# One root for two norms, and activation rows at one byte distance from the weights, in a fused two-model kernel

## The chip, the cores and the metric

The kernel runs on one core of a Trainium2 chip, in one launch. The metric is device time in microseconds, the median of several runs; lower is better.

## The reference

Two small transformers run one after the other on 256 tokens of width 1024, in float32. The first has two layers: MLA and stick-breaking attention in layer 0, chunked band attention in layer 1, each followed by a SwiGLU of inner width 2816, and at the end its final norm. The second puts 16 meta tokens in front (272 columns), has one layer with a gated depthwise convolution and a sparse attention side by side, and then an FFN with a 3-tap convolution. What matters here:

```python
def rms_norm(x, g):
    return x * rsqrt(mean(x * x) + EPS) * g

def reference(...):
    x = first_block(...)          # ends in rms_norm(h, g_final)
    return second_block(x, ...)
def second_block(x, meta_tokens, ...):
    stream = concat([meta_tokens, x])
    h = rms_norm_2(stream, mix_norm_g[0])
    proj = h @ w_in[0]
    ...
    stream = stream + (g_a * y_a + g_b * y_b) @ w_merge_out[0]
```

So between the last down projection of the first model and the first projection of the second lie two norms in a row: the final norm, whose result also is the residual stream, and the mixer's norm of that stream.

## The kernel before, in words

Activations are kept transposed: 8 k tiles of 128 features by 256 (or 258, or 272) tokens. Every product is made of three fp32r matmuls, in `product` (L541 to L543): high part of the weights by high part of the activations, high by low, low by high. Weights come in units of 256 output columns, 8 k tiles of 1024 bytes a partition: SyncE loads a unit into one of four `raw` slots, ScalarE rounds it to `w_hi` (L364), VectorE subtracts to get `w_lo` (L380; in the mixer POOL does so in four parts, L392), two units ahead of TensorE. A unit takes 48 matmuls, 2 tiles by 8 k tiles by 3; a down unit 36 or 30.

The stages stand in the program one after another and each engine has its own stream, ordered by hand in numbered slots: block 0 (in-projections and attention, out-projection, 22 gate/up units, 16 down units), block 1 likewise with 12 QKV units, then the mixer (25 units), `wo`, `pw`, `merge`, 22 FFN units, 16 down units. In the stages whose functions are `ffn_pe` and `down_pe` TensorE runs products without other work between; in the attention stages short steps of the attention are put between every few k tiles.

Activation operands are `u_hi`, `u_lo` (gate/up, QKV, mixer, `pw`, `merge`), `a_hi`, `a_lo` (down), `o_hi`, `o_lo` and `o3_hi`, `o3_lo` (out-projections of blocks 0 and 1), `lat_hi`, `lat_lo` (MLA latents). Between the last down stage of block 1 and the mixer the streams are: `residual_dve` scales and adds the down tiles to `h` (L812, L817), ScalarE squares them (L858), POOL folds two of four pairs (L467), TensorE sums over features with a matrix of ones (`square_sums`, L476), ScalarE makes the root by Ln and Exp (L431, L434), VectorE norms `h` in place (L517), ScalarE squares the eight rows again (L418), TensorE sums those (`norm_pe`, L450), ScalarE makes the second root, and VectorE and ScalarE then make `u_hi` and `u_lo` tile by tile (L517, L443, L510), the first mixer unit following tile by tile.

Where tiles lie in a partition follows from the sizes in order of allocation, each rounded up to 32 bytes. Modulo 256 bytes all weight tiles start at 128. The rows that are the moving operand lie:

| operand | row pitch before | start before | distance from the weights before | pitch after | distance after |
|---|---|---|---|---|---|
| `u_hi`, `u_lo`, 256 columns | 1088 | 128 | 0, 64, 128, 192, then again | 1024 | 192 |
| the same, 258 and 272 columns | 1088 | 128 | as above | 1280 (`m_hi`, `m_lo`) | 192 |
| mixer, query and gate units | 1088 | 184 | 56, 120, 184, 248 | 1280 | 248 |
| mixer, "qi" units | 1088 | 192 | 64, 128, 192, 0 | 1280 | 0 |
| `o_hi`, `o_lo`, `o3_hi`, `o3_lo` | 1024 | 192 | 64 | 1024 | 192 |
| `a_hi`, `a_lo` | 1024 | 64 | 192 | 1024 | 192 |
| `lat_hi`, `lat_lo` | 1024 | 64 | 192 | 1024 | 192 |

In some units (values of attention) the activations are the stationary operand and the weights move.

## Time and profile before

| | |
|---|---|
| median of 3 runs | 1136.59 us (1134.62 to 1137.52) |
| the profiled execution, time | 1133.53 us |
| its span | 1131.7 us |
| TensorE matmul busy | 1092.2 us, 97% |
| VectorE, ScalarE, POOL busy | 66%, 51%, 19% |
| three lines of `product`, `u` operands | busy 517.2, 510.7 and 510.2 us, 1800 matmuls each |
| stages (us from the span's start) | block 0 in 11 to 132, out-projection to 143, gate/up to 270, down to 330; block 1 attention to 450, gate/up to 577, down to 637; mixer 650 to 846; wo, pw, merge to 926; FFN 932 to 1060, down to 1121 |

Matmuls overlap: one lasts some 280 ns while the next begins after some 118 ns, so the time of a stage is the number of its matmuls by the spacing of their starts, and the duration of one is a finer gauge of the same thing. A window of the trace that lies inside a stage gives the spacing: its length by the matmuls in it.

### The profile page before, as it was taken

To read this page: it belongs to the slowest core of one execution; us is meant where nothing else is said; L and a number is where in the kernel's file an instruction comes from. 1 tells how busy PE (TensorE), PEld (TensorE's weight loads), DVE (VectorE), ACT (ScalarE), POOL (GpSimd) and SP (SyncE) were. 2 spreads that over 40 slices of the span, in tenths; PEclk is the share of its full clock that TensorE was granted. 3 is DMA by queue.
4 is the path that set the end of the run, shared out by engine and by line. 5 is a ranking of instruction groups with operands and counts; after the bars stand their busy time and mean duration, and the time that the engine had idled before them with its cause. 6 is when DMAs were issued, how large, how long until landed. Compare 5 with 4: busy or idle time off the path is not lost.

```text
span 1131.7 us, 22236 instructions
## 1 busy us (share of the span) xinstructions
PE 1092.2 (97%) x8781; PEld 1064.6 (94%) x8781; DVE 748.5 (66%) x1229; ACT 577.6 (51%) x847; POOL 215.5 (19%) x198
## 2 busy tenths in 40 slices
PE   7998999999999999999999799999999989999998
PEld 7997899999999999999999799998899989999997
DVE  6776566555657776556555549997886647788653
ACT  5666554444544564544444444446666346655542
POOL 1432030000222110300000067775550000000000
PEclk9999999999999999999999989999999999999999
DMA  8744256555775433566456534454335444465461
GB/s 265 212 114 136 74 179 194 185 167 186 231 242 178 141 122 112 163 200 194 153 182 200 155 112 149 133 167 126 102 122 174 149 149 150 150 197 174 133 201 38
DMA packets 187925, 181.36 MB, mean 160 GB/s; under 512 B 17935, under 2 KB 186268, under 8 KB 187851
## 3 DMA queue, kind: packets, MB, share of 16 engines
q1 hardware_dynamic: 187323, 178.23, 50.0%
q0 software_dynamic: 528, 2.10, 0.6%
q8 instruction: 51, 0.84, 0.3%
q14 instruction: 23, 0.19, 0.1%
HBM read 179.27 MB, written 1.05 MB: 159 GB/s over the span
## 4 chain that ended last, share of the span: by engine, by line
PE 87%; ACT 5%; DVE 3%; POOL 3%; issue 2%; DMA 0%; SPq 0%; ACTq 0%; POOLq 0%; DVEq 0%
PE ps L541 26%; PE ps L542 26%; PE ps L543 26%; POOL work L467 2%; ACT w_hi L364 2%; POOL w_lo L392 1%; PE ps L2008 1%; PE ps L2070 1%; PE ps L450 1%; PE ps L1890 1%; PE ps L2077 0%; PE ps L1897 0%; DVE work L517 0%; DVE w_lo L380 0%; PE ps L1909 0%
## 5 line engine op out<-in xcount | busy, mean ns | idle before, releaser
L541 PE MATMUL ps<-u_hi,w_hi 128*128 128x256 f32 (+2 forms) x1800 | 517.2, 287 | 13.9 <-DVE u_lo L510 6.9
L542 PE MATMUL ps<-u_lo,w_hi 128*128 128x256 f32 (+2 forms) x1800 | 510.7, 284 | 0.0
L543 PE MATMUL ps<-u_hi,w_lo 128*128 128x256 f32 (+2 forms) x1800 | 510.2, 283 | 0.0
L380 DVE TENSOR_TENSOR w_lo<-raw,w_hi 128x2048 fp32r<-128x2048 f32 (+3 forms) x157 | 326.5, 2090 | 143.6 <-ACT w_hi L364 143.3
L541 PEld LDWEIGHTS ps<-u_hi,w_hi 128*128 128x128 f32 x1800 | 343.1, 191 | 17.2 <-issue 13.3
L543 PEld LDWEIGHTS ps<-u_hi,w_lo 128*128 128x128 f32 x1800 | 343.2, 191 | 0.0
L542 PEld LDWEIGHTS ps<-u_lo,w_hi 128*128 128x128 f32 x1800 | 342.5, 190 | 0.8
L364 ACT ACTIVATE w_hi<-raw 128x2048 fp32r<-128x2048 f32 (+3 forms) x182 | 316.3, 1753 | 39.6 <-PE ps L543 29.7
L541 PE MATMUL ps<-a_hi,w_hi 128*128 128x256 f32 x528 | 146.0, 276 | 0.0
L542 PE MATMUL ps<-a_lo,w_hi 128*128 128x256 f32 x528 | 145.9, 276 | 0.0
L543 PE MATMUL ps<-a_hi,w_lo 128*128 128x256 f32 x528 | 145.8, 276 | 0.0
L392 POOL TENSOR_TENSOR w_lo<-raw,w_hi 128x512 fp32r<-128x512 f32 (+1 forms) x100 | 125.2, 1284 | 80.1 <-ACT w_hi L364 63.5
L467 POOL TENSOR_TENSOR work<-work 128x512 f32<-128x512 f32 (+1 forms) x15 | 30.5, 2032 | 542.0 <-ACT work L858 444.7
L541 PEld LDWEIGHTS ps<-a_hi,w_hi 128*128 128x128 f32 x528 | 99.1, 188 | 0.2 <-DVE w_lo L380 0.2
L542 PEld LDWEIGHTS ps<-a_lo,w_hi 128*128 128x128 f32 x528 | 99.2, 188 | 0.0
L543 PEld LDWEIGHTS ps<-a_hi,w_lo 128*128 128x128 f32 x528 | 99.1, 188 | 0.0
L2481 DVE SCALAR_TENSOR_TENSOR ps<-cin,conv_w,ps 128x256 f32<-128x256 f32 x224 | 92.6, 480 | 0.0
L541 PE MATMUL ps<-o_hi,w_hi 128*128 128x256 f32 (+1 forms) x192 | 56.2, 293 | 1.5 <-POOL w_lo L392 0.7
L542 PE MATMUL ps<-o_lo,w_hi 128*128 128x256 f32 (+1 forms) x192 | 54.0, 281 | 0.0
L543 PE MATMUL ps<-o_hi,w_lo 128*128 128x256 f32 (+1 forms) x192 | 54.0, 281 | 0.0
L910 ACT ACTIVATE a_hi<-act_a 128x512 f32 (+1 forms) x22 | 13.9, 632 | 66.5 <-DVE act_a L934 66.5
L858 ACT ACTIVATE work<-h (+2 forms) x32 | 12.0, 413 | 69.9 <-DVE h L817 69.7
(327 smaller groups left out, 1311.1 us busy)
## 6 DMA issues: line engine op xcount, KB each, us to landing
raw<-in_w_in SPq DMA_DIRECT2D x24, 1024.0 KB, 5.3
raw<-in_w_gate SPq DMA_DIRECT2D x22, 1024.0 KB, 5.3
raw<-in_w_up SPq DMA_DIRECT2D x22, 1024.0 KB, 5.4
raw<-in_ffn_up SPq DMA_DIRECT2D x22, 1024.0 KB, 5.1
raw<-in_w_down SPq DMA_DIRECT2D x16, 768.0 KB, 4.4
raw<-in_od_w_qkv SPq DMA_DIRECT2D x12, 1024.0 KB, 5.2
raw<-in_w_down SPq DMA_DIRECT2D x16, 640.0 KB, 4.2
raw<-in_ev_w_in SPq DMA_DIRECT2D x7, 1024.0 KB, 10.1
```

Of the source, the lines that this page charges most:

```text
L364: nc.scalar.activation(w_hi[t % RING][:, 0:n], raw[t % RAW][:, 0:n], ACT.Copy).then_inc(hi_done, 1)
L380: nc.vector.tensor_tensor(w_lo[t % RING][:, 0:n], raw[t % RAW][:, 0:n], w_hi[t % RING][:, 0:n].bitcast(F32), ALU.subtract).then_inc(lo_don ...
L392: a = nc.gpsimd.tensor_tensor(w_lo[t % RING][:, cols], raw[t % RAW][:, cols], w_hi[t % RING][:, cols].bitcast(F32), ALU.subtract)
L450: mm = nc.tensor.matmul(ps[:, bank, 0:n], ones, work[:, kt, 0:n], start=kt == 0, stop=kt == nk - 1)
L467: nc.gpsimd.tensor_tensor(first, first, paired(work)[:, j, :, 0:n], ALU.add).then_inc(sem("sq_folded"), 1)
L541: nc.tensor.matmul(out_ap, a_h, b_h, start=start and n == 0, stop=False)
L542: nc.tensor.matmul(out_ap, a_h, b_l, start=False, stop=False)
L543: mm = nc.tensor.matmul(out_ap, a_l, b_h, start=False, stop=stop and n == len(pairs) - 1)
L858: nc.scalar.activation(paired(work)[:, j, t, 0:n], paired(h)[:, j, t, cols], ACT.Square)\
L910: nc.scalar.activation(paired(a_hi)[:, j], act_a[:, s], ACT.Copy).then_inc(sem("ffn_hi"), 1)
L1890: nc.tensor.matmul(ck_bank(n)[:, P:CK_W], q_pad_c[:, n % 4, P:T1], k_c[:, n // 2, :], start=True, stop=True)\
L2481: nc.vector.scalar_tensor_tensor(out=ends if w == taps else own, in0=cin[:, tile, w + META:w + T2], scalar=conv_w[:, tile, w:w + 1], in1=e ...
```

## The change

It has two parts.

Layout. `u_hi` and `u_lo` get rows of 256 columns (1024 bytes); the same memory is used under other names, `m_hi` and `m_lo`, with rows of 320 columns (1280 bytes) wherever 258 or 272 columns are used. Small unused tiles (`u_place`, `scope_place`, `o_place`, `o3_place`) shift starts so that the distances of the table result. To make room, `x_root` and `q_pad` and two of the 16 heads of the bias table go to the leftovers of the `m` rows, `cva` and `cvb` to `work`, `ki` to `rstd`, `first_cols` to `log_ms`; `act_g` and `act_a` become halves of `acts`.

```diff
+U_PITCH, U_SHIFT = 320, 48
+SHIFT = 16
...
-    u_hi = sb("u_hi", [P, KT, T2], F32R)
-    u_lo = sb("u_lo", [P, KT, T2], F32R)
+    sb("u_place", [P, U_SHIFT])
+    with ExitStack() as t:
+        u_hi = sb("u_hi", [P, KT, T1], F32R, scope=t)
+        hi_rest = sb("hi_rest", [P, KT * (U_PITCH - T1)], scope=t)
+        u_lo = sb("u_lo", [P, KT, T1], F32R, scope=t)
+        lo_rest = sb("lo_rest", [P, KT * (U_PITCH - T1)], scope=t)
+    m_hi = sb("m_hi", [P, KT, U_PITCH], F32R)
+    m_lo = sb("m_lo", [P, KT, U_PITCH], F32R)
...
+    sb("scope_place", [P, SHIFT])
...
+        sb("o_place", [P, 2 * SHIFT], scope=s)
...
+        sb("o3_place", [P, 2 * SHIFT], scope=s)
...
     def u_h(n):
-        return lambda kt: u_hi[:, kt, 0:n]
+        return lambda kt: (u_hi if n == T1 else m_hi)[:, kt, 0:n]
```

Norms. The sum over squares is taken once, of `h` before the final norm with the final gain in the square's scale; its root, with epsilon squared added, gives the mixer's input from `h` directly, with the product of both gains. The plain root and the normed `h` are made too, behind the mixer's input. Meta tokens, which have no final norm, are handled in 16 columns of their own.

```diff
         def squares(j, t):
+            if ph is ph_down1:
+                nc.scalar.activation(paired(work)[:, j, t, META:T2], paired(h)[:, j, t, cols], ACT.Square,
+                                     scale=root_scale[:, bass.ds(j * 2 + t, 1)]).then_inc(sem("sq_done"), 1)
+                return
...
+                for t in range(2 if ph is ph_down1 else 0):
+                    nc.scalar.activation(paired(acts)[:, j, t, :], paired(h)[:, j, t, cols], ACT.Square)\
+                        .then_inc(sem("plain_sq"), 1)
...
-        fold_squares("final", T1)
+        fold_squares("mix2", T2)
+        for j in (1, 2):
+            pool.wait_ge(sem("plain_sq"), 2 * j + 2)
+            wait(pool, sem("plain_folded"), j - 1)
+            first = paired(acts)[:, 0]
+            nc.gpsimd.tensor_tensor(first, first, paired(acts)[:, j], ALU.add).then_inc(sem("plain_folded"), 1)
...
+        nc.scalar.activation(root_scale[:], gains[:, at:at + KT], ACT.Square).then_inc(sem("scale_step"), 1)
+        act.wait_ge(sem("scale_step"), 1)
+        nc.scalar.activation(root_scale[:], root_scale[:], ACT.Ln, bias=eps[:, 0:1]).then_inc(sem("scale_step"), 1)
+        act.wait_ge(sem("scale_step"), 2)
+        nc.scalar.activation(root_scale[:], root_scale[:], ACT.Exp, scale=0.5).then_inc(sem("scale_step"), 1)
+        act.wait_ge(sem("ffn_lo"), 2 + FFN["ffn1"] + FT // 2)
+        nc.scalar.activation(work[:, :, 0:META], h[:, :, 0:META], ACT.Square).then_inc(sem("scale_step"), 1)
+        act.wait_ge(sem("scale_step"), 4)
         residual_act(ph_down1, C1, group=4)
-        norm_finish_act("final", KT, C1, D)
-        for kt in range(KT):
-            act.wait_ge(sem("un_done"), norm_at["final"][1] + kt + 1)
-            square(h[:, kt, :], kt, T2)
-        norm_finish_act("mix2", KT, C2, D, (u_h(T2),))
...
+        both_roots()
+        norm_round_act(norm_at["mix2"][1], KT, T2, u_h(T2))
+        plain_root()
...
-        square_sums("final", T1)
-        pe.wait_ge(sem("rstd_done"), norm_at["final"][0] + 1)
-        norm_pe("mix2", KT, T2)
+        square_sums("mix2", T2)
+        pe.wait_ge(sem("plain_folded"), 2)
+        pe.wait_ge(sem("plain_sq"), KT)
+        pairs_read(pe, ph_down1)
+        for n, kt in enumerate((0, 1, KT - 2, KT - 1)):
+            mm = nc.tensor.matmul(ps[:, 6, 0:T1], ones, acts[:, kt, :], start=n == 0, stop=n == 3)
+        mm.then_inc(sem("ss_done"), 1)
...
-        norm_dve("final", h_at(C1), ("final", 0), KT, T1, into=h_at(C1))
-        dve.wait_ge(sem("un_done"), norm_at["final"][1] + KT)
-        norm_dve("mix2", h_at(C2), ("mix2", 0), KT, T2, (u_h(T2), u_l(T2)))
```

VectorE, from the end of the down stage to the mixer's first steps, before:

```order
L517 SCALAR_TENSOR_TENSOR h<-h,gains,rstd 128x256 x8
L517 SCALAR_TENSOR_TENSOR work<-h,gains,rstd 128x272 x2
L510 TENSOR_TENSOR u_lo<-work,u_hi 128x272
L517 SCALAR_TENSOR_TENSOR work<-h,gains,rstd 128x272
...
L510 TENSOR_TENSOR u_lo<-work,u_hi 128x272 x2
L2497 TENSOR_TENSOR cin<-ps,sg 128x272 x2
```

The same place after the change (`m_lo` takes the place of `u_lo`, and `log_ms` holds the plain root):

```order
L2529 TENSOR_TENSOR work<-meta_gained,rstd 128x8x16
L2531 SCALAR_TENSOR_TENSOR work<-h,both_gains,rstd 128x256 x2
L2524 TENSOR_TENSOR m_lo<-work,m_hi 128x272
L2531 SCALAR_TENSOR_TENSOR work<-h,both_gains,rstd 128x256
...
L2524 TENSOR_TENSOR m_lo<-work,m_hi 128x272 x2
L2539 SCALAR_TENSOR_TENSOR h<-h,gains,log_ms 128x256 x8
L2577 TENSOR_TENSOR cin<-ps,sg 128x272 x2
```

The eight norms of `h` moved from ahead of the mixer's input to behind it, and stand now in front of the first `cin`; one small multiplication for the meta columns was added.

ScalarE at the same place, before:

```order
L431 ACTIVATE log_ms<-ps,eps 128x256
L434 ACTIVATE rstd<-log_ms 128x256
L418 ACTIVATE work<-h 128x272 x8
L431 ACTIVATE log_ms<-ps,eps 128x272
L434 ACTIVATE rstd<-log_ms 128x272
L443 ACTIVATE u_hi<-work 128x272 x8
L364 ACTIVATE w_hi<-raw 128x1088
```

After, with the sigmoids of the first unit's tiles (`sg`) at the end:

```order
L1482 ACTIVATE log_ms<-ps,eps 128x256
L1483 ACTIVATE log_ms<-ps,eps 128x16
L1486 ACTIVATE rstd<-log_ms 128x272
L456 ACTIVATE m_hi<-work 128x272 x8
L1492 ACTIVATE log_ms<-ps,eps 128x256
L1495 ACTIVATE log_ms<-log_ms 128x256
L377 ACTIVATE w_hi<-raw 128x1088
L1523 ACT_TABLE_LOAD
L1523 ACTIVATE sg<-ps 128x272 x2
```

The eight squares in the gap are gone, and one Ln and Exp moved behind the rounding, ahead of the next split and the sigmoids.

## Rows read from the trace of the kernel before

**Rows 1.** The page: the span; busy time, share and instructions of each engine.
```profile
span 1131.7 us, 22236 instructions
...
PE 1092.2 (97%) x8781; PEld 1064.6 (94%) x8781; DVE 748.5 (66%) x1229; ACT 577.6 (51%) x847; POOL 215.5 (19%) x198
```

**Rows 2.** Windows: block 0 gate/up, block 0 down, second model's gate/up.
```profile
core 0: us, PE busy (x) PEld busy (x) DVE busy (x) ACT busy (x) POOL busy (x), PEclk, DMA share, GB/s
160.00:260.00 100.00, 100.00 (x850) 100.00 (x849) 59.29 (x46) 43.90 (x36) 0.00 (x0) 1.00 0.54 169
272.00:322.00 50.00, 50.00 (x443) 50.00 (x442) 31.83 (x33) 26.05 (x28) 8.56 (x4) 1.00 0.73 235
...
937.00:1057.00 120.00, 120.00 (x1003) 120.00 (x1001) 93.96 (x122) 71.61 (x85) 0.00 (x0) 1.00 0.51 164
```

**Rows 3.** Line L542 by window: count, duration ns min/median/max, first and last start us.
```profile
L542 PE MATMUL ps<-lat_lo,w_hi x26: 276/276/283, 77.5 to 93.8; 128*128 128x256 f32 x26
...
L542 PE MATMUL ps<-o_lo,w_hi x29: 280/280/280, 132.8 to 142.7; 128*128 128x256 f32 x29
...
L542 PE MATMUL ps<-u_lo,w_hi x283: 274/282/283, 159.8 to 259.7; 128*128 128x256 f32 x142
...
L542 PE MATMUL ps<-a_lo,w_hi x147: 276/276/276, 272.0 to 321.7; 128*128 128x256 f32 x147
...
L542 PE MATMUL ps<-u_lo,w_hi x334: 277/282/294, 937.0 to 1056.9; 128*128 128x258 f32 x167
...
L542 PE MATMUL ps<-a_lo,w_hi x24: 277/281/281, 1060.5 to 1068.6; 128*128 128x256 f32 x24
...
L542 PE MATMUL ps<-a_lo,w_hi x148: 276/276/276, 1069.9 to 1119.9; 128*128 128x256 f32 x148
```

**Rows 4.** The chain that ended last, from the first sums to the mixer: start, us, what.
```profile
638.93 1.15 PE ps L476 x4
640.08 0.02 issue
640.10 0.48 ACT log_ms L431
...
640.61 0.42 ACT rstd L434
...
642.15 5.61 PE ps L450 x16
...
648.74 0.03 issue
...
650.42 0.36 PE ps L541
```

**Rows 5.** Timeline of VectorE, the final norm of `h`.
```profile
641.06 3.25 DVE L517 SCALAR_TENSOR_TENSOR h<-h,gains,rstd 128x256 f32<-128x256 f32 x8 [2.48 <-ACT rstd L434]
```

**Rows 6.** Windows: a stretch of the second sums.
```profile
642.50:645.90 3.40, 3.40 (x9) 2.59 (x8) 1.81 (x5) 2.27 (x6) 0.00 (x0) 0.50 0.02 5
```

**Rows 7.** Matmuls by line and form over the whole run: busy us, mean ns.
```profile
L542 PE MATMUL ps<-u_lo,w_hi 128*128 128x256 f32 x976 | 275.2, 282 | 0.0
...
L542 PE MATMUL ps<-u_lo,w_hi 128*128 128x258 f32 x672 | 191.7, 285 | 0.0
...
L543 PE MATMUL ps<-u_hi,w_lo 128*128 128x272 f32 x152 | 43.9, 289 | 0.0
...
L542 PE MATMUL ps<-o_lo,w_hi 128*128 128x256 f32 x128 | 35.9, 281 | 0.0
...
L542 PE MATMUL ps<-w_lo,u_hi 128*128 128x256 f32 x112 | 31.4, 280 | 0.0
```

**Rows 8.** Timeline of VectorE and ScalarE at the mixer's second unit.
```profile
659.75 0.44 DVE L2497 TENSOR_TENSOR cin<-ps,sg 128x272 f32<-128x272 f32 x1 [4.30 <-PE ps L543]
...
657.29 0.69 ACT L1469 ACTIVATE sg<-ps 128x272 f32<-128x272 f32 x2
```

**Rows 9.** Timeline of VectorE, the first splits of block 1's down stage.
```profile
581.29 4.56 DVE L380 TENSOR_TENSOR w_lo<-raw,w_hi 128x1280 fp32r<-128x1280 f32 x3 [1.90 <-ACT w_hi L364]
```

**Rows 10.** Timeline of VectorE at the end of the mixer.
```profile
843.93 0.87 DVE L2481 SCALAR_TENSOR_TENSOR work<-cin,conv_w,ps 128x256 f32<-128x256 f32 x2
...
852.30 0.70 DVE L2657 TENSOR_TENSOR gates<-ps,gates 128x516 f32<-128x516 f32 x1 [2.21 <-PE ps L543]
```

118 lines of the change are left out of this document (82 added, 36 removed).

## The prediction

> **What bounds the kernel now.** Start with the page: TensorE is busy in 97% of the span, at a granted clock near full; VectorE has a third of its time free, ScalarE a half [rows 1]. So two things can shorten this kernel: fewer nanoseconds per matmul, and fewer microseconds in which TensorE has no product to work on.
>
> For the first, read windows that lie inside one stage. A window counts about two matmuls more than begin in it. In the first block's gate/up stage 848 begin in 100 us, 117.9 ns from one to the next; in its down stage 441 in 50 us, 113.4 ns; in the last gate/up stage, with 258 columns instead of 256, 1001 in 120 us, 119.9 ns [rows 2]. Clock 1.00 in all three, weights of the same form, both engines of the split with room. DMA is busier in the quicker stage (0.73 against 0.54), so DMA isn't what slows the other.
>
> Then look at single matmuls. In the down stage every one lasts 276 ns; in gate/up the median is 282; the first out-projection has 280 for all; the 26 of the latent stage go from 276 to 283 with a median of 276; the last down stage opens at 281 and is at 276 later [rows 3]. A duration stands 163 ns above its spacing, so 276 is 113.4 and 281 is 118. What differs is where the moving rows lie. By the table above, rows of `a_hi` and `lat_hi` keep 192 bytes (modulo 256) from the weights; those of `u_hi` step through 0, 64, 128, 192 with the k tile; those of `o_hi` keep 64. The 276 appears without scatter in long stages only at the constant 192. But the last down stage opens in the 118 ns rhythm at that same distance: the constant 192 makes the 113 ns rhythm possible and does not guarantee it.
>
> For the second, the chain of waits between the first model's last down stage and the last mixer: sums end at 640.08, the final norm's root is made, eight rows of `h` are normed and squared, eight sums follow, a second root, and the first product starts at 650.42 [rows 4, 5]. A clock of 0.50 lies over 3.4 us of those sums [rows 6].
>
> **The change, term by term.**
>
> *256-column products of gate/up, blocks one and two.* 2 stages x 22 units x 48 = 2112 matmuls, at distance 192 with rows of 1024 bytes, as in the down stage. 117.9 - 113.4 = 4.5 ns each, 9.5 us. Down stages spent about 72 of 1584 matmuls in the 118 ns rhythm (24 x 3 in the last one's opening [rows 3]), so I take 95%: **9.0 us**.
>
> *Their other 256-column products.* The table has 976 x 3 = 2928 with `u` moving [rows 7]; less the 2112 and the 96 of the mixer's "qi" units, which start 64 bytes on and come to distance 0, 720 remain, worth 3.2 us. With `o_hi` and `o3_hi`, moved from 64 to 192, come 384 more [rows 7]: 1.7 us. Both run between attention steps, like the latent stage, where the median says that at least half are at 276. Between a half and all I take two thirds: 3.3 us.
>
> *258 columns.* 672 x 3 = 2016 [rows 7]. In the last gate/up stage, the conv output and the merge, 1440 rows start at distance 192. Two columns more at 2.4 GHz are 0.8 ns, so 114.2 against 119.9: 5.7 ns, 8.2 us, 95% of it 7.8 us. The other 576 (query and gate units) start 56 bytes on, at 248. No row shows a constant 248; bounds are 0 and 3.3 us. The nearest row is the constant 64 of the out-projection, which is at 280 [rows 3], so 0.
>
> *272 columns.* 152 x 3 = 456 at 289 ns (spacing 126) [rows 7]; in the quick rhythm they would be 113.4 + 16/2.4 = 120.1. 5.9 ns each, 2.7 us, two thirds: 1.8 us.
>
> *Products with the weights moving.* 336 [rows 7]. What moves, the weights, now lies 64 bytes ahead of what stands still, as the moving rows do in the out-projection at 280 ns: 0, at most 336 x 4.5 = 1.5 us.
>
> *The norms.* Down-stage scaling, residual adds and the last squares stay, so sums still end at about 640.1. Then Ln twice (0.48 and, for 16 columns, at most as much again; half of it taken), Exp 0.42: root at 641.3 [rows 4]. One small multiplication (0.3), then the path of today from root to first product, 648.74 to 650.42 = 1.7 us: 643.3. That is 7.1 us sooner [rows 4]. The low clock came at 642.5 while TensorE was sparse; in the new order that moment lies at the end of an idle gap just before the first unit. If it comes, half of 3.4 us is lost on products instead of sums. The first unit is paced by VectorE, so some is hidden: **6.0 us**, bounds 5.4 and 7.1.
>
> *What takes the place of the moved steps.* The eight norms of `h` (3.25 us [rows 5]) now stand behind the last `m_lo` on VectorE, in front of the first `cin`. There VectorE waits 4.30 us for TensorE today [rows 8], so they cost nothing; if TensorE is 4% quicker about half a microsecond of that wait is left. ScalarE gets a Ln and Exp (0.9 us) before the first sigmoid, which frees the bank for the second unit's second tile: today the sigmoids end by 657.98 with the first at 657.6, TensorE needs it when the first `cin` can start, 659.75 [rows 8]. A slack of 2.1 us becomes about 1.1, so this costs nothing. The four plain sums run on TensorE from 640.1, at the 1.15 us per four records of their neighbour 2.3 us [rows 4], inside the wait for the root. Ahead of the down stage ScalarE does three operations of 8 elements and one of 128, after the last `a_lo`; about 1 us. The first split there is complete a third of 4.56 us after 581.29, at 582.8, and TensorE ends two units of 36 matmuls, begun at 577.1, at 585.3 [rows 9]: of 2.5 us of slack 1.5 are left, cost nothing. The bias table's second DMA and mask run on POOL, busy 19% [rows 1], during block 0's down stage, and are wanted in the attention after it: nothing. Convolution ends on VectorE at 844.80, 7.5 us before the unit whose product frees the next step at 852.30 [rows 10]; a mixer quicker by 3 to 5 us leaves that covered.
>
> Sum: 9.0 + 3.3 + 7.8 + 1.8 + 6.0 = 27.9 us. The profiled execution took 1133.5 us, 3.1 less than the median of the runs; 1105.6 against it, **1108.7** against the median 1136.6.
>
> **Rivals.**
>
> *A. The layout does nothing.* The difference could belong to the stages. For: the out-projection has 280 with a constant distance too; the last down stage's opening has 281 at 192. Against: 276 ns flat against a spread of 274 to 283 under equal clock and less DMA [rows 2, 3]. It would leave the norms alone: 1136.6 - 6.0 = 1130.6. The Trainium skill, "TensorE: Matmul & The Clock Gate", section on what each phase is for, says so in effect: "Loading the next tile's weights doesn't steal SBUF read bandwidth from the running matmul." By that sentence the bytes between weights and moving rows could not matter. Rows 3 don't bear it out. Chance 0.11.
>
> *B. One or both long stages fall into the 118 ns rhythm and stay.* The last down stage did so until its first pause. The 256-column stages would lose 9.0 us (1117.7), the 258-column ones 7.8 less the 1.6 that 118.8 against 119.9 still gives (1114.9), both together 1124. Chance 0.14.
>
> *C. More than forecast.* All at 276, distances 248 and reversed included, norms at 7.1: 9.5 + 3.2 + 1.7 + 8.2 + 3.3 + 2.7 + 1.5 + 7.1 = 37.2 us, 1099.4. Chance 0.04 to come near it.
>
> *D. Slower.* In the last gate/up stage single matmuls reach 294 ns, 12 above the median [rows 3], and the view does not say at which distance. If a constant distance pins the 2016 258-column rows at a bad phase instead of a good one, and 256 columns gain nothing, the price at 8 ns each is 16 us against 6.0: 1146.7. It is slower beyond the noise from 4.7 ns per row ((6.0 + 3.4) / 2016). Chance 0.04.
>
> **How the numbers follow.** Forecast 0.65 (1100 to 1114), B 0.14, A 0.11, C 0.04, D 0.04, and 0.02 that A meets a lost sigmoid slack and ends where it began. A change is told from none at 0.3%, 3.4 us. Faster: 0.65 + 0.14 + 0.11 + 0.04 = 0.94; same 0.02; slower 0.04. The range goes from C's edge, 1099, to 1127, past both stages of B; A, D and the last case, 0.17, are left out.
>
> **What would show it.** Windows inside gate/up with 113 to 114 ns spacing and 276 ns flat; 258-column matmuls at 277; the first mixer product some 3.2 us after the sums end, 10.3 now [rows 4]; no new wait of TensorE on a sigmoid or on `cin`. Wrong: 282 ns in gate/up (A), a stage flat at 281 (B), 258-column rows above 285 (D).

## The result, and where the time went

The changed kernel takes 1121.97 us (median of four runs, 1120.33 to 1123.33); the kernel before, beside it, 1137.05 (1134.62, 1136.59, 1137.52 and one of 1341.13). The ratio is 0.9876, with a 95% interval of 0.9856 to 0.9895: 14 to 15 us sooner. I had forecast 28. Executions more than 1.5% above the fastest of their kernel, like that one, 1140.01 us of `e2_layout` and 1133.01 us of `e11_anchor`, stay out of the ratios, and no reading below rests on them. The profiled execution took 1122.15 us, 11.4 less than the profiled one before; the shares of the engines are almost those of before [rows 1].

The page of the changed kernel, its span and first line:

```profile
span 1120.4 us, 22257 instructions
...
PE 1083.7 (97%) x8773; PEld 1057.2 (94%) x8773; DVE 753.0 (67%) x1233; ACT 578.6 (52%) x852; POOL 220.8 (20%) x202
```

The windows of the changed kernel: block 0 gate/up, block 0 down, block 1 gate/up, block 1 down, the last gate/up with 258 columns (columns as in [rows 2]):

```profile
158.00:262.00 104.00, 104.00 (x920) 104.00 (x920) 62.06 (x49) 46.67 (x40) 0.00 (x0) 1.00 0.54 170
272.00:322.00 50.00, 50.00 (x444) 50.00 (x443) 33.99 (x33) 23.61 (x25) 7.45 (x4) 1.00 0.79 252
460.00:568.00 108.00, 108.00 (x919) 108.00 (x919) 63.19 (x50) 47.89 (x40) 0.00 (x0) 1.00 0.54 170
575.00:625.00 50.00, 50.00 (x427) 50.00 (x426) 28.73 (x26) 24.32 (x27) 6.33 (x4) 1.00 0.58 187
925.00:1045.00 120.00, 120.00 (x995) 120.00 (x995) 93.79 (x121) 70.39 (x84) 0.00 (x0) 1.00 0.51 164
```

Single matmuls of the product's second line (the third row [rows 3] is its counterpart) in the same five windows:

```profile
L555 PE MATMUL ps<-u_lo,w_hi x306: 276/276/276, 158.1 to 261.8; 128*128 128x256 f32 x153
L555 PE MATMUL ps<-a_lo,w_hi x148: 276/276/276, 272.0 to 321.9; 128*128 128x256 f32 x148
L555 PE MATMUL ps<-u_lo,w_hi x306: 281/281/281, 460.1 to 567.8; 128*128 128x256 f32 x153
L555 PE MATMUL ps<-a_lo,w_hi x142: 281/281/281, 574.9 to 624.7; 128*128 128x256 f32 x142
L555 PE MATMUL ps<-m_lo,w_hi x332: 280/283/289, 924.9 to 1044.9; 128*128 128x258 f32 x166
```

Read them together, with two matmuls taken off each count as in the prediction. (From here on a product is one matmul.) Block 0 is what was forecast: 104 / 918 = 113.3 ns from one product to the next, 117.9 before, every duration 276. Block 1 has the same code and the same distance of 192 bytes and stands at 108 / 917 = 117.8 ns, every duration 281. Its down stage, 113.4 before, is at 50 / 425 = 117.6: the pace went over from gate/up without a break. The 258-column stage has no flat duration at all and is at 120.8 ns, against 119.9 before.

The chain that ended last, between the first model's last down product and the mixer (start, us, what), to be laid beside [rows 4]:

```profile
632.07 0.13 PE ps L556
...
634.12 1.20 PE ps L489 x4
635.34 0.47 ACT log_ms L1482
635.81 0.17 ACT log_ms L1483
636.01 0.44 ACT rstd L1486
...
638.31 0.36 PE ps L554
```

From the end of the sums, 635.32, to the first product it is 3.0 us; before, 10.3 [rows 4]. This part came out as worked out, and a little better.

By the first starts of the stages, the 11.3 us between the two spans come from: everything up to block 0's long gate/up stretch (mainly the o products and the opening turn) 1.7 us; that stretch 4.5; block 0's down nothing; the attention after it and block 1's opening 0.9; block 1's gate/up stretch 0.2; its down stage **2.3 lost**; the norms 7.2; the mixer to the merge 0.7; the last gate/up stage **1.3 lost**, and 0.3 lost at the very end. The clock stood at 0.50 for 6.8 us around the start of that stage, where it had stood there for 3.4; the stage's products ran under it for 4.3 us instead of 3.4, which at half the clock is about 0.4 us of the loss. The rest is within what this stage varies by: in fourteen profiles with its code and place unaltered it took 128.1 to 130.4 us, here 129.6, and 128.3 before.

### The profile page after: what moved, and what is told of

The parts are those of the page before. It is cut to its first block, busy times and chain, and to the rows that moved or that the text cites. A ratio compares the mean times of both kernels' runs of the same rounds, so it can differ in the third digit from the quotient of the medians.

```text
span 1120.4 us, 22257 instructions
## 1 busy us (share of the span) xinstructions
PE 1083.7 (97%) x8773; PEld 1057.2 (94%) x8773; DVE 753.0 (67%) x1233; ACT 578.6 (52%) x852; POOL 220.8 (20%) x202
## 4 chain that ended last, share of the span: by engine, by line
PE 87%; ACT 5%; DVE 4%; POOL 3%; issue 2%; DMA 0%; SPq 0%; ACTq 0%; POOLq 0%; DVEq 0%
PE ps L554 26%; PE ps L556 26%; PE ps L555 26%; POOL work L480 2%; ACT w_hi L377 1%; POOL w_lo L405 1%; DVE w_lo L393 1%; PE ps L1944 1%; PE ps L2128 1%; PE ps L2066 1%; PE ps L1951 1%; PE ps L2135 1%; PE ps L1964 0%; PE ps L1963 0%; PE ps L2090 0%
## 5 line engine op out<-in xcount | busy, mean ns | idle before, releaser
L554 PE MATMUL ps<-u_hi,w_hi 128*128 128x256 f32 x944 | 265.9, 282 | 3.7 <-DVE w_lo L2285 2.4
L556 PE MATMUL ps<-u_hi,w_lo 128*128 128x256 f32 x944 | 263.6, 279 | 0.0
L555 PE MATMUL ps<-u_lo,w_hi 128*128 128x256 f32 x944 | 263.5, 279 | 0.0
L554 PE MATMUL ps<-m_hi,w_hi 128*128 128x258 f32 (+2 forms) x856 | 250.2, 292 | 9.2 <-DVE m_lo L523 4.2
L556 PE MATMUL ps<-m_hi,w_lo 128*128 128x258 f32 (+2 forms) x856 | 245.2, 287 | 0.0
L555 PE MATMUL ps<-m_lo,w_hi 128*128 128x258 f32 (+2 forms) x856 | 245.2, 286 | 0.0
L556 PEld LDWEIGHTS ps<-u_hi,w_lo 128*128 128x128 f32 x944 | 178.2, 189 | 0.0
L554 PEld LDWEIGHTS ps<-m_hi,w_hi 128*128 128x128 f32 x856 | 165.0, 193 | 11.5 <-issue 10.6
L555 PEld LDWEIGHTS ps<-m_lo,w_hi 128*128 128x128 f32 x856 | 165.0, 193 | 0.6
L556 PEld LDWEIGHTS ps<-m_hi,w_lo 128*128 128x128 f32 x856 | 164.9, 193 | 0.0
```

Source lines behind the costliest of these rows:

```text
L554: nc.tensor.matmul(out_ap, a_h, b_h, start=start and n == 0, stop=False)
L555: nc.tensor.matmul(out_ap, a_h, b_l, start=False, stop=False)
L556: mm = nc.tensor.matmul(out_ap, a_l, b_h, start=False, stop=stop and n == len(pairs) - 1)
```

## The experiments

Each of the two blocks has the same plan of products. Its opening is two gate/up units of 48 products; then come sums for the norm (the late sums), for which TensorE waits; then 20 gate/up units and the down stage, 960 + 528 = 1488 products without other work between, called the long stretch. In the program the first four units (the opening turn) are written out, sixteen are four turns of a loop, and two follow it. Where one time is given for an experiment, that kernel ran once.

Theory P, formed on this trace: at a constant distance of 192 a stream of 256-column products keeps one of two rhythms, 113.3 ns (276) or 117.8 ns (281), from its entry until something interrupts it, and 258 or 272 columns never reach either. Its rivals: S, the norm part of the change slows block 1; L, the rhythm belongs to the place in the program; K, any constant distance would do as well as 192. P leaves open what chooses; most of the runs are about that. "Rhythm" below is one of these two; a number alone, 276 or 281, names it.

### The two halves of the change

`e1_norms` is the kernel before with the new norms alone, `e2_layout` the changed kernel with the old norms.

```diff
 e1_norms: the kernel before, plus
+                          ("ffn1", KT, KT), ("mix2", KT, KT), ("final", 0, 0), ("ffn2", KT, KT), ("final2", KT, KT)):
...
 e2_layout: the changed kernel, with
...
-        square_sums("mix2", T2)
+        square_sums("final", T1)
+        pe.wait_ge(sem("rstd_done"), norm_at["final"][0] + 1)
+        norm_pe("mix2", KT, T2)
```

> The kernel before with the norm part of the change alone; its layout is untouched. Theory P (at a constant distance from the weights the long streams of products keep one of two rhythms, 113.3 or 118 ns, that is set where the stream begins; the norms are a separate gain): the gap between last down product and first mixer product falls from 13.3 to about 6.1 us, every stage of products keeps its spacing, time 7 us under the kernel before (about 1130). Rival S (the mixer's norms are what slowed block 1's gate/up and down stages, by their extra work on ScalarE and POOL): block 1's down stage goes from 113.3 to 118 ns here as well, and the gain is about 4 us.

> The changed kernel with the norm part undone, layout kept. P: block 0 gate/up at 113.3 ns as in the changed kernel; block 1 gate/up and down at either 113.3 or 118, each flat (nothing but the state at the entry decides, and this kernel's instructions up to there are the same, so most likely 118 again); 258-column stages near 120; time 7 us over the changed kernel, about 1129. S: with the norm part gone block 1 gate/up and down are at 113.3, and the time is about 1122, no worse than with both parts.

Measured: the norms alone 1126.98 us (1126.21 to 1129.33), ratio 0.9926 (0.9902 to 0.9949). The layout alone 1130.57, but nine of its ten times run from 1122.62 to 1138.82, ratio 0.9944 (0.9913 to 0.9974); the kernel before had a median of 1136.02 beside them.

The chain of `e1_norms` at the join:

```profile
638.97 1.20 PE ps L479 x4
...
643.16 0.36 PE ps L544
```

Windows of `e2_layout` in block 0's and block 1's gate/up:

```profile
160.00:264.00 104.00, 104.00 (x885) 104.00 (x884) 61.27 (x48) 45.88 (x38) 0.00 (x0) 1.00 0.55 169
466.00:570.00 104.00, 104.00 (x886) 104.00 (x884) 60.89 (x49) 47.04 (x40) 0.00 (x0) 1.00 0.55 172
```

The first mixer product comes 3.0 us after the sums here too, 643.16 against 650.42: 7.3 us for the norms by the trace, and the interval of the ratio (5.8 to 11.1 us) holds it. In the layout kernel both blocks stand at 104 / 883 = 117.8 ns, without any of the norm work, and in `e1_norms` block 1's down stage takes 59.9 us as before, so S falls. P's own expectation missed too: it gave block 0 of the layout kernel 113.3 ns again. And a kernel whose only new part is a place in memory has times that spread over 16 us, with mean granted clocks of 0.985 and 0.984 in the quickest and the slowest of the nine: the layout makes the time a matter of something that differs between executions.

### The same kernel again

```diff
 e5_again: no edit
```

> The changed kernel once more, unaltered, over five rounds. Theory P: at one distance modulo 256 a stream of 256-column products holds one of two rhythms (276 ns a product and one start per 113.3 ns, or 281 ns and one per 118), and which one is drawn anew in every execution at each break of the stream. Then the profile need not repeat the first one's stages: each of the two blocks (gate and up plus down, 1488 products) stands wholly at 113 to 114 or wholly at 118 ns, a block at 118 costs 1488 x 4.6 ns = 6.8 us, and the single times spread over at least 7 us, in clumps near 1115, 1122 and 1129 us. Rival L (the rhythm belongs to the place in the program): block 0 at 113.7 and block 1 at 118.1 again, and the times within 3 us of 1122.

Measured: 1121.83 us, ratio 0.989 (0.9864 to 0.9916); the six times are 1120.21, 1121.18, 1121.67, 1121.98, 1122.12 and 1129.42. Single matmuls of this execution in block 0 and block 1:

```profile
L555 PE MATMUL ps<-u_lo,w_hi x295: 281/281/281, 160.0 to 263.9; 128*128 128x256 f32 x148
L555 PE MATMUL ps<-u_lo,w_hi x306: 276/276/276, 466.1 to 569.8; 128*128 128x256 f32 x153
```

It is the first profile turned round: block 0 at 281, block 1 at 276. L falls. A block of 1488 products at 281 instead of 276 costs 6.6 us by the stages' times, 113.3 against 109.0 in gate/up and 62.2 against 59.8 in down (the expectations say 6.8). With the first four, ten executions: nine between 1120.2 and 1123.3, one 7 us above, none 7 us below. Two of the ten were profiled, and their code up to there ran in three more profiles: block 0 at 281 and block 1 at 276 in `e3_kick` (ahead of its first added product) and `e7_narrow`, both at 281 in `e2_layout`. So it is most likely, by the times, that nearly always one block is at 276 and one at 281, more often than two independent draws of even odds would have it; why they go opposite ways stays open. The mean granted clock doesn't sort the ten: it was 0.989 in the one of 1129.42 and 0.987 to 0.994 in the others. Smaller steps come from it: the products of the convolution's output and the merge took 50.4 us where the clock stood at 0.50 for 3.4 us in them, as in the first profile, and 48.8 where it did not, as in this one. The last down stage varies as well, 60.5 us in most profiles and 62.5 in three, where it stood at 281 for most of its length.

### Breaking the stream by one product

`e3_kick` puts one product of 16 columns ahead of each of the four looped turns of block 1's gate/up, `e6_widths` one of changing width ahead of every unit of those turns in both blocks.

```diff
 e3_kick
+            if name == "ffn1" and k == 0 and not isinstance(i, int):
+                wait(nc.tensor, pair_read[0], ph.used_before(i, 0))
+                nc.tensor.matmul(ps[:, 0, 400:416], ones, ones[:, 0:16], start=True, stop=True)
 e6_widths
...
+        kicks = {"ffn0": (16, 64, 128, 256), "ffn1": (32, 48, 96, 192)}.get(kicked)
+            nc.tensor.matmul(ps[:, 2 * p, 256:256 + kicks[k]], ones, work[:, 0, 0:kicks[k]], ...)
```

> The changed kernel with one product of 16 columns, whose result nobody reads, in front of the first unit of each loop turn of block 1's gate/up stage (4 times). P: each is a break of the stream and draws the rhythm anew, so that stage shows stretches of 192 products, each flat at 113.3 or flat at 118; if all four fall to 113.3 from the first on, gate/up and the down stage behind it gain up to 6 us less the cost of the four (about 0.2 us each). Rival L (the rhythm belongs to the stage: to what block 1's other engines do or to where its code lies): the stage stays at 118 throughout but for the products next to the added ones.

> The changed kernel with one more product ahead of every unit in the looped turns of gate and up: 16, 64, 128 and 256 columns wide in the four units of a turn of block 0, and 32, 48, 96 and 192 in block 1 (40 added products; their sums go to columns that nobody reads). Theory P: each of the 40 pieces of 48 products is wholly 276 or wholly 281 ns, and both kinds come up in both blocks; if the added product only shifts the phase, its width decides which change of rhythm follows, so that pieces behind one width go one way and not half and half. Rival: a break does nothing by itself and the rhythm of the block returns behind every one. Time 1122 us and 40 x 0.15 to 0.3 us more, with up to 4.4 us to either side by the pieces.

Measured: `e3_kick` 1124.55 us. Single matmuls behind its four added products:

```profile
L555 PE MATMUL ps<-u_lo,w_hi x62: 281/281/281, 474.8 to 496.3; 128*128 128x256 f32 x62
L555 PE MATMUL ps<-u_lo,w_hi x61: 276/276/276, 497.9 to 518.3; 128*128 128x256 f32 x61
L555 PE MATMUL ps<-u_lo,w_hi x61: 281/281/281, 520.0 to 541.2; 128*128 128x256 f32 x61
L555 PE MATMUL ps<-u_lo,w_hi x81: 276/276/276, 542.8 to 570.0; 128*128 128x256 f32 x81
```

Every piece is wholly one or the other, and each added product turned it over; the last piece kept its 276 through the down stage (53 / 468 = 113.2 ns, some 814 products on). `e6_widths` took 1128.13 us. Its 32 pieces of 48 products (the looped turns are four; I had counted 40 pieces) alternate without exception. Two neighbours, behind 16 and behind 64 columns:

```profile
L555 PE MATMUL ps<-u_lo,w_hi x16: 281/281/281, 166.6 to 171.9; 128*128 128x256 f32 x16
L555 PE MATMUL ps<-u_lo,w_hi x16: 276/276/278, 172.5 to 177.6; 128*128 128x256 f32 x16
```

So the rhythm isn't drawn at each break, as I had thought: in a running stream one added product leads to a definite one. What the run can't separate, since the widths stood in a fixed order, is whether a width always turns the rhythm over or always leads to the same one; only 16 columns are seen from both sides (`e3_kick`: 276 to 281 twice and 281 to 276 twice).

### Other distances

`e4_dist0`, `e8_dist64` and `e12_dist128` move only the rows of the normed activations.

```diff
-U_PITCH, U_SHIFT = 320, 48
-SHIFT = 16
+U_PITCH, U_SHIFT = 320, 0      e8_dist64: 16     e12_dist128: 32
+SHIFT, O_SHIFT = 64, 32        e8_dist64: 48     e12_dist128: 32
...
```

> The changed kernel with the rows of u and m at distance 0 from the weights instead of 192 (a and o rows stay at 192). P with the distance mattering: at a constant 0 gate/up of block 0 is no longer at 113.3 but at some other flat value, 116 to 120; the down stages keep their two rhythms. Rival K (any constant distance with 1024-byte rows gives the two rhythms; only the change of distance from row to row cost time): gate/up of blocks 0 and 1 flat at 113.3 or 118 as at 192.

> The changed kernel with the rows of the normed activations at distance 64 instead of 192 from the weights modulo 256; gated activations stay at 192. With distance 0 (the run before) these products stood at 120.0 ns, all at 283 ns. If the distance alone sets a speed and 192 is a good one, 64 gives a flat stage too with a duration of its own: by the o products of the kernel before, which stand at distance 64 with 279 to 280 ns, 116 to 118 ns a product. If any constant distance other than 0 does, it is 113.3 or 118 by the draw.

> The rows of the normed activations at distance 128 from the weights modulo 256, all else as in the changed kernel: the last of the four distances that rows of 1024 and 1280 bytes at steps of 64 can take. 0 gave 120.0 ns a product in every stretch, 64 117.8, 192 113.3 or 118. If 192 is the only one with a short rhythm, 128 stands between 117 and 120; if there are two kinds of distances it shows 113.3 in one block at least. Time by that 1122 to 1131 us.

Measured: 1132.29, 1126.13 and 1129.30 us. In block 0's gate/up, windows from 160 to 264, at distance 0, 64 and 128:

```profile
160.00:264.00 104.00, 104.00 (x869) 104.00 (x869) 60.38 (x47) 46.06 (x40) 0.00 (x0) 1.00 0.54 167
160.00:264.00 104.00, 104.00 (x886) 104.00 (x885) 61.33 (x48) 45.88 (x38) 0.00 (x0) 1.00 0.54 169
160.00:264.00 104.00, 104.00 (x879) 104.00 (x878) 60.99 (x48) 46.36 (x39) 0.00 (x0) 1.00 0.54 170
```

That is 120.0, 117.6 and 118.6 ns a product. Weight loads are rows of their own; those of the first line of `product`, at distance 0, then (changed kernel) at 192 in the 276 and in the 281 rhythm:

```profile
L553 PEld LDWEIGHTS ps<-u_hi,w_hi x290: 192/192/192, 159.8 to 263.9; 128*128 128x128 f32 x145
```
```profile
L554 PEld LDWEIGHTS ps<-u_hi,w_hi x307: 187/188/188, 157.8 to 261.9; 128*128 128x128 f32 x154
L554 PEld LDWEIGHTS ps<-u_hi,w_hi x307: 192/192/192, 459.8 to 568.0; 128*128 128x128 f32 x154
```

At distance 0 the loads of all three lines take 192 ns and every product 283. At 192 in the 281 rhythm the loads of the first line take 192 and the others 188; in the 276 rhythm all take 188. So the place of the rows does matter, by up to 6.7 ns a product. The weight loads beside the products go with it only in part: at 64 they take 187 to 188 ns, as in the 276 rhythm, under products of 279 and 280, and at 128 they take 187 to 189 under products of 279 to 285. Both blocks are alike at 0, at 64 and at 128, none of them has the 276, and their down stages, still at 192, have it in five cases of six. K falls; of the four distances 192 is the only one with a short rhythm.

All these runs move the activation rows and leave the weights at 128, so the rows' own start (modulo 256) could be what matters, and not the distance. The units for the values of attention tell the two apart: there the weights move, always from 128, and the activations, which stand still, lie elsewhere in each kernel. Their second matmul up to 90 us, in the changed kernel (moving rows 64 ahead of those that stand), in `e4_dist0` (0), `e8_dist64` (192 ahead) and `e12_dist128` (128):

```profile
L555 PE MATMUL ps<-w_lo,u_hi x32: 278/279/280, 24.9 to 76.7; 128*128 128x256 f32 x32
L554 PE MATMUL ps<-w_lo,u_hi x32: 278/283/283, 26.2 to 79.1; 128*128 128x256 f32 x32
L555 PE MATMUL ps<-w_lo,u_hi x32: 276/281/281, 24.9 to 77.0; 128*128 128x256 f32 x32
L555 PE MATMUL ps<-w_lo,u_hi x32: 278/281/287, 26.3 to 78.9; 128*128 128x256 f32 x32
```

The moving rows start at the same place in all four, and the durations follow the distance: 279 to 280 at 64, 283 at 0, 276 or 281 at 192, scattered at 128. By the activations' own start it would be the other way round: at 64 they give 276 or 281 where they move and 279 to 280 where they stand. So it is the distance between the two operands.

### 256 columns in the last gate/up stage

The last two of the 258 columns are left out of these products (they belong to the last two tokens; the two extra columns that the 3-tap convolution needs stand first), so this kernel computes something else and serves only to time the stage.

```diff
+            if name == "ffn2":
+                n, xh, xl = T1, (lambda kt: m_hi[:, kt, 0:T1]), (lambda kt: m_lo[:, kt, 0:T1])
```

> The changed kernel, whose third block's gate and up products read and write 256 columns instead of 258 (the last two halo columns are left out of these products; the rows stay 1280 bytes apart). Theory P: the 258 columns are what keeps this stage from a rhythm, so with 256 it stands at 113.3 or at 118 ns a product, flat at 276 or 281 ns, in place of 122.9, and ends 5 to 10 us sooner. Rival L: the stage is held by its own code (the loop, the work beside it), and stays at 121 to 122 ns a product, 1 ns less for the two columns at most, or 1 us.

Measured: 1112.10 us. The stage goes from 129.6 to 121.4 us. Its window and a line of its products:

```profile
925.00:1035.00 110.00, 110.00 (x973) 110.00 (x972) 92.50 (x121) 67.91 (x83) 0.00 (x0) 1.00 0.55 179
```
```profile
L555 PE MATMUL ps<-m_lo,w_hi x324: 276/276/276, 925.0 to 1034.9; 128*128 128x256 f32 x162
```

110 / 971 = 113.3 ns, flat, in the same loop beside the same work of the other engines: two columns fewer are worth not 0.8 ns but 7.5. This is the other half of P, and the term that failed by most: 258 columns find no rhythm at 192. Nor elsewhere: by the stage's time over its 1056 products, breaks included, they took 121.5, 120.6 and 123.6 ns at distances 0, 64 and 128 (one profile each), 121.3 to 123.5 in the fourteen profiles at 192, and 121.5 before. Why two columns more should keep a stream from either rhythm, no run shows.

### Chains of products, and pauses

`e9_chains` has several added products ahead of the units, `e10_pause` makes every second unit wait until VectorE has read the one before.

```diff
 e9_chains
+        heads, sums = (P, P, 256, 256), (256, 256, P, P, P)
+        kicks = {"ffn0": ((16, 16), (P, P), heads, sums), "ffn1": (heads, (16,), heads, (16, 16, 16))}.get(kicked)
 e10_pause
+            if k % 2 == 1:
+                nc.tensor.wait_ge(pair_read[ph.pair(k - 1)], ph.used_before(i, k - 1) + 1)
```

> The widths run showed that one added product turns the rhythm over behind it, 276 to 281 ns or back, 40 times of 40 and at every width. Here the looped turns of gate and up have whole chains of added products ahead of their four units: in block 0 two of 16 columns, two of 128, (128, 128, 256, 256) and (256, 256, 128, 128, 128); in block 1 (128, 128, 256, 256), one of 16, (128, 128, 256, 256) and three of 16. Theory T (each added product turns it over): two and four of them keep the rhythm, one, three and five turn it. Theory E (the last products ahead of the stream set its rhythm, whatever it was): the chain (128, 128, 256, 256), which stands ahead of the o products, where every execution so far entered at 276 ns, gives 276 ns each time, from either rhythm, and would be a way to hold the short one. Time: about 27 us of added products (by 110 ns for each 16 or 128 columns and 216 for 256), so some 1149 us by either.

> Breaks by waiting alone: in the looped turns of gate and up, every second unit waits until VectorE has read the unit before it (about 1 us of idle TensorE, 20 pauses); in block 1 the units between have one added product of 16 columns ahead, so that the pauses meet both rhythms. If a pause leaves the rhythm as it is or always gives the same one, the pieces behind the 20 pauses show it. Theory P as first told: behind a pause either rhythm comes, about half and half, in both blocks. Time 1122 + 20 x 0.8 to 1.2 us, about 1142 us.

Measured: 1153.29 and 1149.74 us. In `e9_chains` (four turns in each block, so 12 of the chain that I had counted 15 times) the same chain is followed by the same rhythm wherever it stands:

| chain | from | to | times |
|---|---|---|---|
| 16, 16 | 276 | 281 | 3 |
| 16, 16 | 281 | 281 | 1 |
| 128, 128 | 281 | 281 | 4 |
| 128, 128, 256, 256 | 281 | 276 | 12 |
| 256, 256, 128, 128, 128 | 276 | 276 | 4 |
| 16 | 276 | 281 | 4 |
| 16, 16, 16 | 276 | 281 | 4 |

The theory that each added product turns the rhythm over (T in the expectations) falls: two of 16 columns led to 281 from either rhythm. A chain is a rule of its own from rhythm to rhythm, and a rule can send both to one; only this chain was seen from both sides here. For the pauses, TensorE's waits in block 0 of `e10_pause` (line waited for: us in total, times, longest):

```profile
PE ps L554 <- DVE acts L858: 9.6, 8, 3.0
```

Eight pauses in each block (16, where I had counted 20), the first of 3.0 us, the others with TensorE idle for 0.8 to 1.1 us. In block 0 the pieces behind them are 281 and 276 without order (the last seven: 281, 281, 276, 281, 276, 276, 281), in block 1, where a product of 16 columns stands between them, the last seven are all 276, the first of these from 276 and six from 281. Idle time can lead either way, even from the same rhythm. But it need not be chance: the six in block 1 that met 281 lasted 782 to 784 ns each, those in block 0 796 to 1113. Length to the nanosecond doesn't settle it either: in block 0, both times coming from 281, a pause of 898 ns led to 281 and one of 897 to 276.

### A fixed chain behind the idle time

```diff
 e11_anchor: two_tiles, opening turn of ffn0 and ffn1, third unit
+            for width in (P, P, 256, 256):
+                nc.tensor.matmul(ps[:, 2 * p, 256:256 + width], ones, work[:, 0, 0:width], ...)
```

> In the chains run the chain (128, 128, 256, 256) was followed by 276 ns 15 times of 15, though the rhythm ahead of it was 281 each time. Here it stands once in each of the first two blocks, behind the late sums of the norm, in front of the third unit of the opening turn; nothing else of the changed kernel is altered. Theory E: both blocks then stand at 276 ns in every execution. Each chain costs 110 + 110 + 216 + 216 = 0.65 us, 1.3 in all; the changed kernel had one block of the two at 281 in most executions, worth 1488 x 4.6 = 6.8 us. So 1122.0 - 6.8 + 1.3 = 1116.5 us, single times within 2 us of each other and none at 1122 or 1129; profile 113.7 ns in both blocks. Rival: behind the idle time of the sums the chain gives either rhythm, and the times stand 1.3 us above the changed kernel's, near 1123, spread like its own.

Measured: 1123.12 us, ratio 0.9868 (0.9839 to 0.9896), times 1115.93, 1122.18, 1122.70, 1123.54, 1123.67 and 1133.01. Block 0 of the profiled execution stands at 281 behind the chain, block 1 at 276:

```profile
160.00:264.00 104.00, 104.00 (x885) 104.00 (x884) 61.12 (x47) 45.04 (x37) 0.00 (x0) 1.00 0.54 169
470.00:570.00 100.00, 100.00 (x884) 100.00 (x884) 59.59 (x46) 44.59 (x37) 0.00 (x0) 1.00 0.56 176
```

The theory that the last added products set the rhythm whatever came before (E in the expectations) falls: behind idle time the chain gives either. Of the times one lies at 1116 and four near 1123, as for both blocks at 276 and for one; the same chain in the same stage of `e9_chains`, in a running stream, had led to 276 twelve times of twelve.

### No idle time ahead of the stream

In each block's opening TensorE waits for POOL's fold of the squares before the late sums. The changed kernel's waits of TensorE in block 0, and in block 1:

```profile
PE ps L497 <- POOL work L480: 1.6, 1, 1.6
```
```profile
PE ps L497 <- POOL work L480: 0.9, 1, 0.9
```

(The expectations below took 1.6 for both.) `e13_mid` puts those sums between the tiles of the third unit, so that TensorE has products to run until POOL is done, and `e14_mid_kick` adds one product of 16 columns behind them in block 0. Theory D in the expectations says that idle time is what makes the draw, and that without it the next rhythm follows from the one before.

```diff
             for t in range(2):
                 mm = feature_tile(outs[t], s, KT, UC, t * P, xh, xl)
+                if t == 0 and sums is not None:
+                    late_sums(sums)
 e14_mid_kick
+                    if sums == "ffn0":
+                        nc.tensor.matmul(ps[:, 2 * p, 256:272], ones, work[:, 0, 0:16], start=True, stop=True)
```

> The late sums of the norm stand between the two tiles of the third unit instead of ahead of it, in the first two blocks, so that 24 products (2.7 us) run while POOL still folds the squares, and TensorE doesn't stand idle there for 1.6 us. Theory D (the draw is made by idle time of TensorE; in a stream without idle time the next rhythm follows from the one before): in block 0 the stretch of o and opening products, 276 ns in every execution so far, is never interrupted by idle time, so block 0 enters its long stretch at one and the same rhythm in every execution. If that is 276 (d1): single times near 1119 and, where block 1 draws 281, 1126, less 3 us, so clumps at 1112 and 1119. If it is 281 (d2): clumps at 1119 and 1126. Rival (something else draws): three clumps 6.8 us apart as before, all of them 3 us lower, most at 1119. All of it: 2 x 1.6 = 3.2 us off the changed kernel's 1122 by the idle time alone.

> As the run before, with one more product of 16 columns behind the moved sums in block 0. Theory D: it turns over what block 0 enters with, so in the profile block 0 stands at the other rhythm than in the run before, and the single times are shifted by 6.8 us the other way; one of the two kernels then has block 0 at 276 ns in every execution and is the best version of all, by 3 to 4 us on the mean of the changed kernel for the draw and 3.2 for the idle time (1115 to 1116 us). Rival: no difference between the two kernels beyond 0.2 us and the draws.

Measured: 1124.65 us (1120.28 to 1127.58), ratio 0.9896 (0.987 to 0.9922), and 1126.18 us (1120.86 to 1128.29), ratio 0.991 (0.9889 to 0.9931). Both clumped less clearly than either theory had it. The wait on POOL was gone, and block 0 and block 1 each went from 276 into 281 behind the moved sums, in both profiles. But then, TensorE's timeline in `e13_mid` (start, us, instruction, idle before and who ended it):

```profile
164.22 0.28 PE L556 MATMUL ps<-u_hi,w_lo 128*128 128x256 f32 x1
164.75 0.36 PE L554 MATMUL ps<-u_hi,w_hi 128*128 128x256 f32 x1 [0.25 <-DVE w_lo L393]
```

The later sums had made the root later, that had held VectorE (4.2 us of waiting for the root, 3.4 in the changed kernel), and now a weight split came late: a pause of 0.25 us. It moves the choice to a new place (281 stayed in `e13_mid`; in `e14_mid_kick`, which entered block 0 at 281 as well, it became 276). The added product of 16 columns turned nothing over here.

`e15_three` and `e16_four` put the sums behind 18 products of that unit, so that the pause goes, and add a chain behind them:

```diff
+                if t == 0 and sums is not None:
+                    feature_tile(outs[t], s, 6, UC, t * P, xh, xl, stop=False)
+                    late_sums(sums)
+                    for width in (128, 128, 128):          e16_four: (128, 128, 256, 256)
+                        nc.tensor.matmul(ps[:, 2 * p + 1, 256:256 + width], ones, work[:, 0, 0:width], ...)
+                    mm = feature_tile(outs[t], s, 2, UC, t * P, xh, xl, x0=6, start=False, w0=6)
+                    continue
```

> The late sums stand behind 18 of the third unit's 48 products, 0.7 us sooner than in e13_mid, with three added products of 128 columns behind them, in both blocks. In e13_mid and e14_mid_kick, where nothing idle preceded the sums, 276 ns turned to 281 behind them four times of four, and a pause of 0.3 to 0.4 us some 8 us later (TensorE waiting for a split of weights, which the later root had delayed) drew anew. In e9_chains five times of five (256, 256, 128, 128, 128) was followed by 276 from 276. Theory D: block 0, which comes in at 276 without idle time, enters at 276 in every execution, and where the pause is gone it stays so to the end; block 1, which opens behind 1.6 us of idle time, keeps its opening rhythm if that is 276. Time: 1122 less 2 x 1.6 for the idle time, plus 2 x 0.66 for the added products, less 6.8 where block 0 was at 281 before: clumps at 1113 to 1114 (both blocks at 276) and 1120, none at 1127. Rival: the pause is still there, and block 0 is drawn as before: all three clumps, 1.9 us below 1115, 1122 and 1129.

> As e15_three with the chain (128, 128, 256, 256) in place of three of 128 columns. In e9_chains it was followed by 276 fifteen times of fifteen, from a stream at 281. Theory D: behind the sums (256, 256) alone 281 follows, and if the chain works on that as it did on a stream at 281, block 0 enters at 276 here too; if it only counts what stands between the streams as a whole, the result may be 281, and then in every execution alike. Either way block 0 shows one rhythm in all executions and the times have two clumps, not three: 1114 and 1121, or 1121 and 1128. Rival: three clumps.

Measured: `e15_three` 1121.11 us (1116.04 to 1123.47), ratio 0.986 (0.984 to 0.9881). `e16_four` 1127.57 us, and its six times are 1126.56, 1127.16, 1127.47, 1127.67, 1127.72 and 1128.07, ratio 0.9931 (0.9916 to 0.9945). Windows of `e16_four` in the two gate/up stages:

```profile
160.00:264.00 104.00, 104.00 (x885) 104.00 (x884) 61.91 (x49) 45.88 (x38) 0.00 (x0) 1.00 0.54 170
470.00:574.00 104.00, 104.00 (x885) 104.00 (x885) 61.19 (x48) 46.24 (x39) 0.00 (x0) 1.00 0.55 173
```

Both at 281, from openings at 276, and six times within 1.5 us, where the changed kernel had spread over 9. This was the level that it reached once in ten (1129.4, less 2.5 us of idle time, plus 1.3 for the chains). The same chain behind idle time, in `e11_anchor`, had left the draw as it was; so it is the missing idle time between opening and long stretch, together with the chain, that makes the rhythm of the blocks the same in every execution, as far as six times and one profile tell. The times of `e15_three` are not the two clumps expected, at 1113 to 1114 and at 1120. It had block 0 at 276 in its profile and block 1, which opened at 281, at 281; but block 0's down stage was broken twice. TensorE's timeline, and ScalarE's waits from 240 to 330 us:

```profile
271.07 0.28 PE L556 MATMUL ps<-a_hi,w_lo 128*128 128x256 f32 x1
271.19 0.39 PE L554 MATMUL ps<-a_hi,w_hi 128*128 128x256 f32 x1
271.41 0.28 PE L555 MATMUL ps<-a_lo,w_hi 128*128 128x256 f32 x1
```
```profile
ACT w_hi L377 <- DMA raw<-in_w_down: 1.8, 3, 1.0
```

ScalarE's waits for the down weights were 1.3 us in two pieces in the changed kernel, where TensorE did not pause there. So a block at 276 that starts its long stretch without the idle time seems to catch up with the down weights' DMAs; and a small pause lets the rhythm go (the 0.22 us from 271.19 to the next start, 0.11 more than in the stream, led to 281 for 131 products).

### Both blocks made to enter at 276

`e16_four`'s way into 281 was safe; one product of 32 columns ahead of the opening turn's fourth unit was to turn it to 276. `e18_plain` has the moved sums and that product, `e17_turned` also the chain of four behind block 1's sums.

```diff
+        if ph in (ph_ffn0, ph_ffn1) and isinstance(i, int) and i == 0 and k == 3:
+            nc.tensor.matmul(ps[:, 2 * p, 256:288], ones, work[:, 0, 0:32], start=True, stop=True)
...
+                    for width in () if sums == "ffn0" else (128, 128, 256, 256):      e18_plain: () in both
```

> e16_four stood at 1126.6 to 1128.1 us in all six executions, with both blocks at 281 ns: its block 1 opened at either rhythm (behind 1.6 us of idle time) and yet entered at 281. So the moved sums and the chain (128, 128, 256, 256) lead to 281 from both. Here one product of 32 columns stands 30 products later, ahead of the opening turn's fourth unit, in both blocks; in the widths run such a product turned 281 to 276 each time (20 of 20 from 281). Block 0 has no chain behind the sums, since 276 went to 281 there without one (four of four). Theory D: both blocks then stand at 276 in every execution: 1127.6 less 2 x 6.8 for the rhythms, less 1.3 for the chain that block 0 lacks, plus 2 x 0.2: 1113.1 us, times within 2 us of each other, and the profile at 113.3 in both blocks except behind pauses, where the weights come late (in e15_three two of 0.1 to 0.3 us in the down products of block 0, which let part of it stand at 281): up to 1116. Rival: the entry isn't fixed, and 1120 or 1127 come up again.

> As e17_turned without the chain in block 1 either, only the moved sums and the product of 32 columns. Block 0 as there. If the moved sums by themselves lead to 281 from both rhythms, block 1 too stands at 276 in every execution, 1.3 us sooner: 1111.8 us, one clump. If they turn the rhythm over instead (276 to 281 and 281 to 276), block 1 is drawn with its opening: two clumps, 1112 and 1119.

Measured: `e17_turned` 1117.01 us (1114.66, 1116.33, 1117.01, 1117.16, 1117.85), ratio 0.9844 (0.9826 to 0.9862); `e18_plain` 1116.58 us (1115.66 to 1120.26), ratio 0.9845 (0.9822 to 0.9867). Windows of `e17_turned` in the two gate/up stages and block 1's down stage:

```profile
160.00:262.00 102.00, 102.00 (x902) 102.00 (x902) 61.09 (x48) 45.80 (x38) 0.00 (x0) 1.00 0.55 173
465.00:565.00 100.00, 100.00 (x884) 100.00 (x884) 60.27 (x47) 43.90 (x37) 0.00 (x0) 1.00 0.57 176
577.00:625.00 48.00, 48.00 (x426) 48.00 (x425) 29.73 (x26) 22.43 (x25) 6.36 (x4) 1.00 0.70 217
```

All at 113.3 ns (the last by 48 / 424 = 113.2). For the first time every execution of a kernel lies at or near the lowest level, and this version is quicker than the changed kernel: 1117.0 against 1121.9, the ranges 1114.7 to 1117.9 and 1120.2 to 1129.4 apart. It is 3.9 us above its forecast of 1113.1 and still 1.0 above the 1116 that I had allowed for pauses; the same waits on down weights stand in it (ScalarE, 2.1 us in three pieces), with one of 0.6 us on TensorE in block 0:

```profile
PE ps L554 <- DVE w_lo L393: 0.6, 1, 0.6
```

In `e18_plain` block 1 opened at 281, the sums led to 276, and the product of 32 columns kept it there; so 32 columns led to 276 from both sides (three entries from 281 and this one from 276), which is the better reading for that width than "turns it over". (In the widths run 32 columns led from 281 to 276 4 times, and all widths together did so 16 times, not 20.) The sums by themselves did turn it over: 276 to 281 four times in `e13_mid` and `e14_mid_kick`, 281 to 276 here. One of the five times of `e18_plain`, 1120.26, stands 2.5 us above the rest.

## Why the prediction was wrong

**The direction and the two mechanisms held, and the size was half.** Worked against the prediction's own terms:

*258 columns, 7.8 us.* **This step failed.** It said that two columns cost 0.8 ns in the quick rhythm and took 95% of the products at 114.2 ns. The stage stayed at 120.8 ns, 0.9 above before. The range of 280 to 289 ns in place of [rows 3]'s 277 to 294 shows it: a narrower spread, but around 283, and neither 276 nor 281 held. `e7_narrow` shows the term at its full size as soon as the products have 256 columns. No row of before had 258 columns at a constant distance; I carried a rhythm seen at 256 columns over to another width, with a formula that only counts columns.

*256 columns of gate/up, 9.0 us.* 4.5 ns a product is right to the tenth, at 113.3 and 117.8. **The 95% was wrong**, and so was that the down stage stays as it is. The sum took the last down stage's opening of 72 products at 281 [rows 3] as a start that passes after some products. It was a stretch that ended at a pause, which rival B had read rightly from the same rows. A stage of 960 + 528 products without a pause keeps what it enters with, and in nine executions of ten, by their times and the two that were profiled, one block of the two entered at 281. That took 4.3 us of the term, and 2.3 more from a down stage that had been at 276 before. That it was one block and not two or none was the draw of the execution; by the runs above, most executions have it so.

*The norms, 6.0 us.* 7.2 by the trace of the whole change, 7.3 by `e1_norms`: the upper bound. The 0.50 clock that I had expected to take a half of 3.4 us on the mixer's first products did not come there; it came at 657.3 us, for 6.7 us as at 669.9 before, and at 916.7. The moved steps cost nothing, as forecast: no wait of TensorE is shown between 640 and 665 us.

*The other 256-column products, 3.3 us.* 1.7 before block 0's long stretch and 0.9 before block 1's: 2.6 us against the 3.3 forecast, a little over half of the 4.9 where two thirds were assumed. The pieces between attention steps are at 276 or 281, one or the other each.

*272 columns, 1.8 us.* The mean duration went from 288 to 287 on the second line, and the whole mixer up to the last gate/up stage gained 0.7 us. The same fault as with 258.

*Rival B* had the right mechanism, at 0.14, and too small a price: it held the long stages' fall to be worth 9.0 for both blocks and did not see that the down stages go with them. Nor were its two halves the same case: for 258 columns there was no rhythm to fall into. *Rival A* is refuted by block 0 and by three other distances. It leaned on a sentence of the Trainium skill, "TensorE: Matmul & The Clock Gate", section "Step-by-step: what each phase is for", that loading the next weights doesn't take SBUF read bandwidth from the running matmul. The measurements differ from what rival A drew from it: the distance alone moves a product from 113.3 to 120.0 ns. Whether read bandwidth is what the two share no run shows, and at 64 the products are slower while their loads are not. *C* and *D* did not come near.

What stays open: why the two blocks go opposite ways in nine of ten executions; by what rule a chain of products leads from one rhythm to the other; whether the length of a pause decides what follows it; and why 258 columns hold no rhythm. The kernel before took 1133.5 us in its profiled execution, under 59 of the 69 times that it ran beside the experiments, and this was most likely a draw of the clock: the 23 with a mean granted clock of 0.989 or more, as that execution had with 0.990, have a median of 1133.8 us, the other 46 one of 1136.8. The 11.4 us between the two profiles are thus 3 less than the difference of the medians.

## What to carry to other kernels

Where products stream without a break, look at the durations one stage at a time: a flat 276 beside a flat 281 on the same code is a property of the execution, and a single profile of such a kernel shows one draw. Take several, and look at how the times clump. A rhythm seen at one width and one distance is a fact about that width and that distance; try the other width by itself before counting on it. And idle time ahead of a long stream can cost more than its length here: with 1.6 and 0.9 us of it gone and no new pause behind, six executions agreed within 1.5 us, and one added product of 32 columns (0.2 us) then chose the short rhythm. In `e13_mid`, where a pause of 0.25 us stood a little later, the times still ran from 1120 to 1128.

## What the runs showed of the hardware

At full clock, with fp32 operands of 128 x 256 and a weight load for each product, the spacing of products in one long stretch was 113.3 ns or 117.8 at distance 192 modulo 256, 117.6 to 117.8 at 64, 118.6 at 128 and 120.0 at 0, without scatter except at 128 (279 to 285 ns). The same durations come with the operands' roles exchanged, by the distance of the moving rows from those that stand (283 ns at 0, 276 or 281 at 192). The rhythm held for some 1535 products and changed only where another instruction or a pause of about 0.1 us or more stood between. In running streams the same added chain led from the same rhythm to the same one in every case seen; behind idle time it led to either. 258 columns took 120.6 to 123.6 ns, breaks included, at all four distances. A fall of the granted clock to 0.50 for 3.4 us inside a stream cost 1.7 us (merge and convolution output, 50.4 us against 48.8).
